# Eight of sixteen gate blocks moved from the attention groups to the stretch of the samples' gather

## What is computed

```
h = modulate(x, norm_mix_g, shift1, scale1)              # adaLN: silu(c) @ w_ada + b_ada, six terms
q, k, v, qi, ki, wi, u, vg, gates = split(h @ w_in)      # gates: 2 x 1024 columns
gate_attn, gate_gmlp = split(sigmoid(gates))
idx   = top_k(index_scores(qi, wi, ki), k)               # samples: 256 of 2049 keys, prompt: 128
attn  = softmax(q . k[idx]) @ v[idx]                     # 8 heads, 2 kv heads; samples gather from paged caches
gm    = u * (W_s vg + b)                                 # chunked causal gMLP
x    += gate1 * ((gate_attn * (attn @ w_proj_attn) + gate_gmlp * (gm @ w_proj_gmlp)) @ w_out)
x    += gate2 * moe(modulate(x, norm_ffn_g, shift2, scale2))   # top-1 of 4 groups, top-2 of 8 experts
```

## The kernel before

**What sets the order.** It is written out by hand, engine by engine. Banks of PSUM are handed over by semaphores: `banks.begin` makes PE wait until the last user of a bank has drained it, `banks.filled` tells the reader. Weights come by SP's queue in the order of `STREAM` into a ring of three slots of 2 MB; entry n goes to slot n % 3, and SP waits for the last use of entry n - 3 before it issues the load:

```
+ [(name, KD * 512) for c in range(4) for name in (f"G{c}", f"ada{4 + 2 * c}", f"ada{5 + 2 * c}")]
+ [("WG", 4 * D), ("WA", 4 * D), ("O0", KD * 512), ("O1", KD * 512)])
```

## Time and profile before

| | us |
|---|---|
| median of 3 runs | 941.94 |
| lowest, highest | 940.84, 942.39 |
| profiled execution, its own time | 939.31 |
| its span | 937.6 |
| PE, PEld busy in the span | 800.6, 466.6 |
| DVE, ACT, POOL busy | 454.2, 182.0, 148.4 |
| mean granted clock of TensorE | 0.932 of full |

### The profile page before, as it was taken

The page is one execution under the profiler, slowest core; times in us unless marked ns, Lnnn a source line. Parts: engine busy times, 40 slices in busy tenths (PEclk is TensorE's granted clock), DMA queues, the critical chain, the costliest instruction groups (busy, mean ns, idle before and its releaser), DMA issues.

```text
span 937.6 us, 10563 instructions
## 1 busy us (share of the span) xinstructions
PE 800.6 (85%) x4024; PEld 466.6 (50%) x4024; DVE 454.2 (48%) x816; ACT 182.0 (19%) x360; POOL 148.4 (16%) x158
## 2 busy tenths in 40 slices
PE   2896998899689999999619999985399999999980
PEld 0153444368556666666417853442255555555540
DVE  1442299568976688883002232174723333333336
ACT  2121223210213333331002010031111111111100
POOL 1110012022000000001740010010223333333310
PEclk9988899999889999999859899997699999999995
DMA  9921022132201524050810231228499999999947
GB/s 357 412 82 57 1 68 85 68 125 89 94 0 44 226 74 196 16 254 5 321 34 1 90 146 64 89 90 343 164 412 423 425 425 428 423 425 424 422 180 274
DMA packets 26218, 184.11 MB, mean 196 GB/s; under 512 B 6788, under 2 KB 7076, under 8 KB 14776
## 3 DMA queue, kind: packets, MB, share of 16 engines
q1 hardware_dynamic: 15192, 159.45, 41.9%
q0 software_dynamic: 10384, 21.86, 6.6%
q10 hardware_dynamic: 592, 2.13, 0.6%
HBM read 179.64 MB, written 14.64 MB: 207 GB/s over the span
## 4 chain that ended last, share of the span: by engine, by line
PE 75%; DVE 8%; DMA 6%; another core or an unknown queue 4%; issue 3%; ACT 3%; DVEq 0%; SPq 0%; POOL 0%; ACTq 0%; POOLq 0%
PE psum L644 20%; PE psum L615 16%; PE psum L1016 12%; PE psum L1030 6%; DMA ring<-in_experts 4%; PE psum L566 3%; DMA ring<-in_stream 2%; PE psum L582 2%; PE psum L1009 2%; PE psum L834 2%; PE psum L817 2%; PE psum L722 2%; ACT arena L1309 2%; PE psum L562 1%
## 5 line engine op out<-in xcount | busy, mean ns | idle before, releaser
L615 PE MATMUL psum<-ring,hT 128*128 128x512 f32 (+2 forms) x384 | 151.1, 550 | 0.0
L644 PE MATMUL psum<-hT,ring 128*128 128x260 f32 x640 | 144.8, 387 | 5.0 <-DVE arena L1747 4.4
L644 PEld LDWEIGHTS psum<-hT,ring 128*128 128x128 f32 x640 | 122.1, 192 | 31.5 <-issue 12.0
L1309 ACT ACTIVATE arena<-psum 128x512 f32<-128x512 f32 (+11 forms) x126 | 68.0, 566 | 349.7 <-PE psum L644 100.3
L615 PEld LDWEIGHTS psum<-ring,hT 128*128 128x128 f32 x384 | 73.4, 195 | 76.8 <-issue 67.6
L644 PE MATMUL psum<-arena,ring 128*128 128x260 f32 x256 | 63.5, 413 | 27.6 <-DVE arena L1801 21.2
L1016 PE MATMUL psum<-ring,arena 128*64 128x256 f32 x672 | 77.9, 385 | 2.2 <-ACT arena L1515 1.6
L1030 PE MATMUL psum<-arena 128*64 128x512 f32 x296 | 71.7, 605 | 2.0 <-issue 2.0
L644 PEld LDWEIGHTS psum<-arena,ring 128*128 128x128 f32 x256 | 52.5, 207 | 38.1 <-DVE arena L1801 21.6
L1016 PEld LDWEIGHTS psum<-ring,arena 128*64 128x64 f32 x672 | 49.5, 139 | 35.4 <-issue 13.8
L1259 POOL DMA_INDIRECT expert_rows<-arena,router x37 | 37.4, 1011 | 150.8 <-DVE arena L2026 150.8
(11 more groups left out here) (315 smaller groups left out, 899.7 us busy)
## 6 DMA issues: line engine op xcount, KB each, us to landing
ring<-in_stream SPq DMA_DIRECT2D x22, 2048.0 KB
ring<-in_experts SPq DMA_DIRECT2D x17, 2048.0 KB
arena<-in_experts SPq DMA_DIRECT2D x32, 1024.0 KB
arena<-in_experts SPq DMA_DIRECT2D x10, 2048.0 KB
hT<-in_experts SPq DMA_DIRECT2D x5, 2048.0 KB
arena<-in_x_prompt POOLq DMA_DIRECT2D x8, 512.0 KB, 9.8
ring<-expert_rows SPq DMA_DIRECT2D x8, 512.0 KB, 6.4
ring<-in_stream SPq DMA_DIRECT2D x2, 1280.0 KB
```

What stands on the lines that cost most here:

```text
L615: mm = pe.matmul(psum[:, b, 0:width], hT[:, k, t * P:(t + 1) * P], w[:, k, :], start=(k == 0), stop=(k == KD - 1))
L644: mm = pe.matmul(psum[:, b0 + s, 0:HALF], w[:, k, f * P:(f + 1) * P], rhs[:, k, s * HALF:(s + 1) * HALF], start=(first and k == 0), stop=( ...
L1309: ins = act.activation(out, in_, func, scale=scale)
```

## The change

Group g keeps one gate block, `gate_block(g)`. Blocks 8 to 15 stand behind the last group; the transposes of the samples' indices come behind block 8, and blocks 9 to 15 behind them. All WG blocks move behind the samples' scores: 0 and 1, and 2 and 3 around the probabilities' transposes, 4 to 7 behind the samples' values. ACT evacuates gate blocks 8 to 15 in one row ahead of the samples' keys, and DVE's products of WG move with the blocks. The transposed probabilities and the new probabilities go to banks 0 and 1 instead of 2 and 3. The stream is in another order, and a table gives the slot of each entry; SP waits for the last use of the entry that held the slot before. The first three experts' gate and up weights and the rows picked at the end lie in other parts of the ring and of `hT`.

```diff
@@ -62,11 +62,16 @@
-          + [(name, KD * 512) for c in range(4) for name in (f"G{c}", f"ada{4 + 2 * c}", f"ada{5 + 2 * c}")]
+          + [(name, KD * 512) for name in ("G0", "ada4", "ada5", "ada6", "ada7", "G1", "ada8", "ada9", "ada10", "ada11",
+                                           "G2", "G3")]
           + [("WG", 4 * D), ("WA", 4 * D), ("O0", KD * 512), ("O1", KD * 512)])
+SLOTS = (0, 1, 2, 0, 1, 2, 0, 1, 2) + (0, 1, 2, 1, 2, 0, 1, 2, 1, 2, 0, 1) + (2, 0, 1, 2)
+REPLACES = {STREAM[n][0]: STREAM[max(m for m in range(n) if SLOTS[m] == SLOTS[n])][0]
+            for n in range(RING, len(STREAM))}
@@ -855,21 +859,17 @@
                 att_values(g)
-                gate_block(2 * g)
-                if g == len(groups) - 1:
-
-                    pe.wait_ge(idx_ready, 1)
-                    banks.begin(pe, "idxT", 4)
-                    for h in range(2):
-                        mm = pe.transpose(psum[:, 4, h * NS:(h + 1) * NS], idx_f[0:NS, h * P:(h + 1) * P],
-                                          ident[0:NS, 0:NS])
-                    banks.filled(mm, "idxT")
-                gate_block(2 * g + 1)
+                gate_block(g)
                 ada_product(4 + g, 6 + (g // NKV + 1) % 2)
 
+            gate_block(8)
+            pe.wait_ge(idx_ready, 1)
+            banks.begin(pe, "idxT", 4)
...
+            for n in range(9, 16):
+                gate_block(n)
@@ -878,8 +877,6 @@
-            gmlp_blocks(0, 1, 2, 3)
@@ -903,20 +901,22 @@
-            gmlp_blocks(4, 5)
+            ring_wait(pe, "WG")
+            pe.wait_ge(gm_ready, 1)
+            gmlp_blocks(0, 1)
             pe.wait_ge(probs_s_ready, 1)
...
-            gmlp_blocks(6, 7)
+            gmlp_blocks(2, 3)
...
+            gmlp_blocks(4, 5, 6, 7)
             ring_wait(pe, "WA")
@@ -1092,8 +1093,9 @@
-                    banks.wait_full(sp, last_use[STREAM[n - RING][0]])
+                    banks.wait_full(sp, last_use[REPLACES[name]])
```

More of the change, by code:

```diff
@@ L439, in decoder_step @@
         hidden_T = at(24576, 4 * SB).rearrange("p (b f n) -> p b f n", b=2, f=2)
-        picked = flat_ring[:, 0:2 * T5 * D].rearrange("p (c t n) -> p c t n", t=T5, c=2)
+        picked = [[ring[:, 2 * c, t * D:(t + 1) * D] for t in range(NT)]
+                  + [hT.rearrange("p k n -> p (k n)")[:, c * D:(c + 1) * D]] for c in range(2)]
         bank_full = [sem(f"bank_full{b}") for b in range(8)]
@@ L857, in _ @@
                 att_values(g)
[L858 to L872 removed]
+                gate_block(g)
+                ada_product(4 + g, 6 + (g // NKV + 1) % 2)
+            gate_block(8)
+            pe.wait_ge(idx_ready, 1)
+            banks.begin(pe, "idxT", 4)
+            for h in range(2):
+                mm = pe.transpose(psum[:, 4, h * NS:(h + 1) * NS], idx_f[0:NS, h * P:(h + 1) * P], ident[0:NS, 0:NS])
+            banks.filled(mm, "idxT")
+            for n in range(9, 16):
+                gate_block(n)
             def gmlp_blocks(*fs):
@@ L1094, in _ @@
                 if n >= RING:
-                    banks.wait_full(sp, last_use[STREAM[n - RING][0]])
-                sp.dma_start(ring[:, n % RING, 0:size], io["stream"][n, :, 0:size]).then_inc(ring_full[n % RING], 16)
+                    banks.wait_full(sp, last_use[REPLACES[name]])
+                slot = SLOT_OF[name]
+                sp.dma_start(ring[:, slot, 0:size], io["stream"][n, :, 0:size]).then_inc(ring_full[slot], 16)
             def expert_src(e):
@@ L1434, in exponentials, with gate_out @@
                 ins.then_inc(exp_ready, 1)
+            def gate_out(n):
+                c, f = n // 4, n % 4
+                to = 2 * c + f if f < 2 else KD + 2 * c + f - 2
+                evac((f"G{c}", f), [(halves(gates[:, to, :]), pair(2 * (f % 2)))], ACT.Sigmoid)
             act.wait_ge(vg_ready, 1)
@@ L1451, in _ @@
                     exponentials(g + 1)
[L1452 to L1455, removed]
+                gate_out(g)
                 if g == 3:
@@ L1461, in _ @@
                 evac(("ada", 4 + g), [(late_G[g], psum[:, 6 + (qb + 1) % 2, :])])
+            for n in range(8, 16):
+                gate_out(n)
             for b in range(NS):
@@ L1820, in _ @@
                .then_inc(probs_s_ready, 1)
-            gmlp_gated(4, 5)
+            gmlp_gated(0, 1)
             banks.wait_full(dve, "new_probs")
-            banks.drained(dve.tensor_copy(sstat[0:NS, 52:60], psum[0:NS, 3, 0:NH]), "new_probs")
+            banks.drained(dve.tensor_copy(sstat[0:NS, 52:60], psum[0:NS, 1, 0:NH]), "new_probs")
             banks.wait_drained(dve, "new_probs")
@@ L1828, in _ @@
                               spread_dim(sstat[0:NS, 52:60], 1, NS), ALU.mult).then_inc(new_spread_ready, 1)
-            gmlp_gated(6, 7)
+            gmlp_gated(2, 3, 4, 5, 6, 7)
             for f in range(KD):
@@ L2067, in _ @@
                     dve.wait_ge(picked_in[c][t], 16)
-                    x, a = x2[0:rows, t, :], picked[0:rows, c, t, :]
+                    x, a = x2[0:rows, t, :], picked[c][t][0:rows]
                     if t == NT:
```

27 lines of the change are left out of this document (13 added, 14 removed).

## The result

The changed kernel took 948.14 us (median of 4 runs, 946.14 to 948.62) where the kernel before took 941.55 us: a ratio of 1.0066, with a 95% interval of 1.0048 to 1.0083. It is slower by 6.6 us. The forecast was 927.8 us, range 920 to 944. The profiled execution has a span of 946.9 us. The median of the kernel before is here that of 4 runs. Lines of the changed kernel differ by a few (L648 is the gate blocks' and WG's line, L1311 ACT's copy out of PSUM, L1752 the first operation of DVE in a group).

A forecast was written before the change was run, and what follows sets the result against it. The prediction took the serial middle as the bound, with PE pacing the attention groups. Its steps brought WA's start from 521.61 to 507.5, 14.1 us off the 941.94 us median, giving 927.8 us; range 920 to 944.

The forecast's parts named there:

- Part 1: Attention groups: one gate block (7.15 us) fewer in each; DVE sets the pace, group 7 starts at 371.9 against 402.46.
- Part 2: Ahead of gate block 8: PE waits 5.3 us for G2's load and loses 2.0 us to slow clock; block ends at 416.6.
- Part 3: Sample gather: index transposes at 416.6 instead of 438.63, so POOL's first gather comes at 420.2 instead of 442.18.
- Part 4: During the gather: PE runs seven gate blocks in 50.05 us, to 466.9; WA blocks start at 507.5.
- the sum: Whole kernel: WA starts at 507.5 against 521.61, 14.1 us gained, giving 927.8 us; chance 0.54 for 922 to 932.
- The rule: Gate blocks during the gather: touched only by PE and ACT, they run at full speed, giving 927.8 us.
- Rival 1: Gate blocks 11 to 15: PE's completions held while POOL gathers; 943.3 us (chance 0.14) or 950.4 us (chance 0.14).
- both its forms: Block 12 first held: 15.5 us lost, 943.3 us, no change; block 11 held too: 22.6 us lost, 950.4 us, slower.
- Rival 2: Groups 4 to 7: clock and waits take 5 to 10 us of gain, 933 to 938 us; chance 0.13, shared with another rival.

The follow-up runs named there:

- a_v_first: The changed kernel with the values gathered first and the keys second, still 32 gathers in a row; 947.36 us (one run).
- a_pauses: The changed kernel with its gathers in four rows of eight, the later rows waiting for gate blocks 11, 13 and 15; 923.96 us (one run).
- b_drain8: The kernel before, with POOL waiting after every eighth gather until all so far have landed; 920.61 us, ratio 0.9787.
- a_drain8: The changed kernel, with POOL waiting after every eighth gather until all so far have landed; 928.09 us, ratio 0.9856.
- a_v_late: The changed kernel, with the sixteen value gathers starting only when gate block 15 is complete; 937.19 us, ratio 0.9972.
- sets 1 and 2: Changed kernel and kernel before with gathers delayed, reordered or broken by pauses; the kernel before beside them took 939.96 and 940.61 us.
- sets 3 to 5: Variants of gather rows, index transposes and ring slots, and both kernels again; the kernel before took 916.64, 916.12 and 916.54 us.
- a_drain12: The changed kernel in rows of 12, 12 and 8 gathers, with a wait for the landing between them; 922.19 us (one run).

## Why the prediction was wrong

**Part 1, the groups: right.** DVE starts groups 2 and 7, and gives the last index, at

```profile
278.94 1.23 DVE L1752 SCALAR_TENSOR_TENSOR arena<-psum,arena 128x1024 f32<-128x1024 f32 x1 [1.90 <-PE psum L821]
...
373.10 2.29 DVE L1752 SCALAR_TENSOR_TENSOR arena<-psum,arena 128x2048 f32<-128x2048 f32 x1
...
398.03 0.28 DVE L1776 TENSOR_SCALAR arena<-arena 8x256 f32<-8x256 f32 x1
```

against 276.9, 371.9 and 397.1. PE waits 2.12, 2.63 and 2.41 us for it ahead of blocks 4 to 6. The slow stretch ahead of block 6 cost 1.6 us of the 1.9 allowed. PE left the groups at 403.2, forecast 402.1.

**Part 2, the load of G2: right.** 5.02 us of wait for 5.3, and block 8 took 9.51 us, 2.4 lost to the clock where 2.0 were set.

**Part 3, the earlier gather: right.** First gather at 421.20, forecast 420.2.

**Part 4, seven gate blocks over the gather: this step failed**, by the whole of the gain and more. The keys' transposes came at 492.04 and not at 466.9, 25.1 us late. The two steps behind it were right again: from there to WA it took 39.2 us (WA at 531.3), where the forecast had 507.5 - 466.9 = 40.6. With the hold absent the step is right to 0.7 us (49.36 for 50.05) and the keys' transposes come at 463.7.

**But the sum would have been wrong there, too.** It credited the change with 21.2 us of PE's idle time ahead of 488.1 in the kernel before. That idle time is the hold; where gate blocks take the place of WG blocks they are held in their turn (the hold cost the kernel before 21.2 us of waiting and 2.2 of slow clock in the block behind, 23.4 us, and the changed kernel 25.0, the keys' transposes at 492.04 instead of 467.1), and where nothing is held there is no idle time to fill. Either way the credit is nil, and what is left is what I had listed against it: waits in the groups and a slower clock. That is why the change costs about the same with the hold and without it, 6.6 us (941.55 to 948.14, interval 4.5 to 7.8) and 6.4 us (916.12 to 922.56, interval 6.0 to 9.4). The gate blocks were work without a gap: in the kernel before, PE is busy for 29.2 to 29.7 of each 30 us from 270 to 420, so taking a block out there can only be repaid by a gap elsewhere.

**The rule.** By the Trainium skill ("SBUF — State Buffer", section "SBUF: two separate sides") TensorE and ScalarE wait for nobody and VectorE alone contends with GpSimd. The sentence is on SBUF's ports, and I had read it as a promise that TensorE runs freely beside the gathers. With the hold present TensorE stands still in the changed kernel while VectorE runs nothing (DVE is idle for 77.3 us, from ahead of the stall until behind it), so VectorE and GpSimd contending for that port pair is not the cause. Without the hold, nothing contradicts the rule. No run shows whether the hold is in SBUF at all.

**The rivals.** Rival 1 named the mechanism, its place and its sign: PE's completions held while POOL gathers, block 11 held, 950.4 us, slower; measured 948.14. I gave it 0.14, and 0.28 for both its forms. The evidence for it was in the earlier trace rows, two completions over 20 us late. The evidence against it, an output emptied on time 7 us into the gather, proved nothing, since the first late completions were due 11 us in and the starts stall some 19 us in. It had block 14 waiting for its banks; in fact PE's starts are held as well, from block 12 on. Rival 2's clock loss was there, at some 2.4 us.

## What to carry to other kernels

Before work is moved into an idle stretch, ask what makes the stretch idle: if it is an unexplained delay of the very engine that is to work there, the moved work waits as well. The gain must then be counted as nil until a run shows that the engine can work in it. And a gap that is counted as a gain should be looked for a second time: here 24 us of 940 came and went with no change of the kernel, while the difference between two kernels timed side by side was 6.6 and 6.4 us, the same within its interval.

Where one engine is busy without a gap, a small sure thing can be worth more than a large move: here the ring slot of one weight (5.2 us of wait and 2.2 us of slow clock) gave 7 us, and the move of eight blocks cost 6.5.

## What the runs showed of the hardware

- **A hold of TensorE during rows of gathers, which comes and goes.** With it, 32 gathers 1.25 us apart in the changed kernel and a_v_first stall TensorE's starts, to one matmul in 0.7 to 2.8 us, from some 19 us after the row's start; completions due 11 us in are already 1.1 and 3.2 us late, and all is over 3 to 5 us after the last issue. By medians of different sets it cost either kernel 23 to 26 us. Rows of eight did not stall the gate blocks, but the samples' scores behind them still reached DVE 5.8 us (a_pauses) and 3.5 us (b_drain8) after their issue instead of 0.2; in a_drain8, whose last row had ended before, they came in 0.2. Rows of 16 did stall them, by 4.8 us in the first row of a_v_late, and held the WG blocks from 10 us on in the second. It was there in the first measurement and in sets 1 and 2, and absent in sets 3 to 5, in 17 runs of the kernel before in each of sets 4 and 5. Sets 1 and 3 bear the same chip number, so it isn't simply a property of one chip.
- What it is stays open. It was not the load of the DMA engines (a share of 0.20 before the stall and in it), nor a fall of the clock (which comes after it), nor which cache is read. Whether the gathers delay the arrival of TensorE's instructions was not tested; by itself that would not explain why blocks already worked off are reported late. Rows of 12, fewer bytes and an earlier row were run only while it was absent, so they tell nothing of it.
- A pause of 5 us on TensorE costs 1.6 to 3.1 us more through the clock: the four WG blocks behind it took 16.48 us against 14.29, and gate block 8 took 8.71 (a_pauses) to 10.29 us (a_drain12) against 7.15.
